# Latents' rows first, the recurrence's first rounds beside the last row chunks, and the input's eight tiles fetched at once

## The chip, the cores and the metric

The program runs on one core of a Trainium2 chip. The metric is the device time of one execution in microseconds (us). Names of engines: PE (TensorE: matmuls and transposes), DVE (VectorE), ACT (ScalarE), POOL (GpSimd), SP (SyncE, which here only issues DMAs). Each engine works off its own instructions in the order in which they were written; semaphores make one wait for another. ACT and POOL issue some DMAs too.

## What is computed

Two transformer blocks in float32 over 1024 tokens of width 1024. The change lies in the first part of the first block alone:

```
mod = silu(c) @ ada_w + ada_b                         # 6 x 1024
sh_m, sc_m, g_m, sh_f, sc_f, g_f = split(mod, 6)
h = rms_norm(x, mix_pre_norm) * (1 + sc_m) + sh_m
proj = h @ w_in                                       # 1024 x 2280
att_p, rwkv_p = proj[:, :456], proj[:, 456:]
y_att  = dsa_attention(c_q, c_kv, idx_k, idx_w ...)   # from att_p; picks the 256 best keys of each row
y_rwkv = rwkv7_group(rwkv_p, ...)                     # a recurrence over the tokens
mix = concat(y_att, y_rwkv) @ w_out
```

Inside `dsa_attention` an index score over all earlier tokens is computed (8 heads, relu, weighted sum), and the 256 largest of each row are kept. Inside `rwkv7_group` each row of `rwkv_p` is mixed with the row before it (`p + mu_shift * (p_prev - p)`), then split into r, k, v (512 columns each) and three narrow inputs of low-rank products (64, 64 and 160 columns, "lora" below), and a state of 8 heads x 64 x 64 is carried over the tokens. Everything behind it (attention proper, the feed-forward layers, the second block) is as before.

## The kernel before, in words

Tokens are worked in 8 tiles (t = 0 to 7) of 128 rows. The stages around the change, in PE's order:

1. **Opening.** `proj_scalar` fetches tiles of x into three buffers `xt`, three at once and each further one when its buffer is free; SP fetches 8 slices of `ada_w` (1 MB each, "mod" steps) into a ring of five slots (`ring_load`, L408). ACT squares and sums a tile, DVE scales it, PE transposes it into `hT` (L528) and multiplies a mod slice (L473). When all eight are through, DVE and ACT scale and shift the rows of `hT` (L724, L960).
2. **Lora**: 48 matmuls of 512 columns (L552) from `hT`; DVE mixes the result with the token before, ACT takes tanh.
3. **att and chunk 0**: per tile 8 matmuls of 256 and 8 of 200 columns (`token_group`, L508) for the attention's latents, then 8 x 8 for the first of six 256-column chunks ("rkv", 0 to 5) of r, k, v.
4. **Turns and index queries** (`LAT_STEPS`), with the first six row steps of chunk 1 between them.
5. **Scores** (`SCORES`, 24 steps): PE makes two heads (L618), ACT takes relu (`rl`, L1019), DVE adds them up (L913).
6. **Row steps** (`ROW_STEPS` from index 6 on): 34 row steps (8 matmuls of 256 columns each, one tile of one chunk) and 16 mod steps, 12 between row steps and 4 behind the last. Beside them DVE and ACT count, for six tiles and 33 candidates, how many scores exceed a candidate (`best_rows`, `best_sums`). That work is cut into 223 steps; `passes_beside` says how many are taken at each row step. Finished chunks go by POOL's DMA to `p_rows` in HBM.
7. **Recurrence.** Behind the last row step SP fetches eight broadcast rows (`rwkv_constants`), waits for the last chunk in HBM, and fetches tile 0 (`rows_load`). All engines meet (`rwkv_start`). Then 82 rounds follow: round g holds round g - 7t of each tile t, of the 33 rounds that a tile has. Rounds 0 to 6 are a tile's front (`front_*`), 7 to 20 its free part (`free_*`), 21 to 32 its part with the state (`state_*`). Beside rounds 0 to 29 two or one steps of `best_rows` are taken (`best_steps`).

## Time and profile before

| | us |
|---|---|
| median of 3 runs | 3683.32 (3676.62 to 3688.82) |
| profiled execution, its own time | 3676.93 |
| its span, first to last instruction | 3675.6 |
| PE busy | 3362.3 (91%) |
| DVE busy | 1789.6 (49%) |
| ACT busy | 931.7 (25%) |
| POOL busy | 345.4 (9%) |

In the page's line of 40 slices PE is at nine tenths or more from the tenth slice (920 us) on, nearly without a break; the slices before it read 6989757888. The attention proper begins at 895.8 us. Only what lies ahead of it is touched.

### The profile page before, as it was taken

The page shows a single profiled execution, that of the slowest core. Times are in us where ns is not written, and L with a number is a line of the kernel's source. Part 1 is how long each engine was busy: PE and PEld are TensorE (multiplying, and loading weights), DVE is VectorE, ACT ScalarE, POOL GpSimd, SP SyncE. Part 2 cuts the span into 40 slices and gives each one's busy share as a digit, 9 for nine tenths or more (in the row PEclk, how much of TensorE's full clock was granted, in tenths as well). Part 3 has the DMA queues.
Part 4 walks back from the last instruction along what each step waited for, and adds up shares of the span by engine and source line. Part 5 has one row for each costly group of instructions (what it writes and reads, how often), then busy time and mean ns, then how long its engine had stood idle before and what let it go on. Part 6 is the DMA issues. An engine that isn't in the chain of part 4 may idle for free.

```text
span 3675.6 us, 51037 instructions
## 1 busy us (share of the span) xinstructions
PE 3362.3 (91%) x21635; PEld 2614.7 (71%) x21650; DVE 1789.6 (49%) x2849; ACT 931.7 (25%) x1710; POOL 345.4 (9%) x277
## 2 busy tenths in 40 slices
PE   6989757888889999999999889999998999999998
PEld 3757546765557788888886556876676888878876
DVE  2248878663566422223544546322246444444556
ACT  2146532332543300001112435000015111111122
POOL 0000156662000000000000000000000000000000
PEclk8999877988999999999999999999999999999999
DMA  6145411110024111112340101101123111123434
GB/s 210 41 68 183 155 36 37 37 60 19 13 75 138 58 46 52 46 50 94 107 140 25 36 24 35 46 21 49 57 98 117 55 47 46 52 69 98 143 113 145
DMA packets 216068, 270.18 MB, mean 74 GB/s; under 512 B 11068, under 2 KB 176226, under 8 KB 215587
## 3 DMA queue, kind: packets, MB, share of 16 engines
q1 hardware_dynamic: 210555, 247.87, 21.1%
q10 hardware_dynamic: 3192, 11.17, 1.7%
q0 software_dynamic: 2096, 7.87, 0.6%
q8 instruction: 173, 2.83, 0.3%
q14 instruction: 52, 0.43, 0.0%
HBM read 232.80 MB, written 34.08 MB: 73 GB/s over the span
## 4 chain that ended last, share of the span: by engine, by line
PE 80%; DVE 11%; ACT 3%; issue 3%; DMA 2%; POOL 1%; SPq 0%; DVEq 0%; ACTq 0%; POOLq 0%
PE psum L1977 18%; PE psum L1981 18%; PE psum L1979 18%; PE psum L508 5%; PE psum L2995 3%; PE psum L1181 2%; PE psum L2495 2%; PE psum L2816 2%; PE psum L2703 2%; PE psum L552 1%; PE psum L1727 1%; PE psum L2832 1%; DVE scores L913 1%; PE psum L1753 1%; DVE Lg L1821 1%
## 5 line engine op out<-in xcount | busy, mean ns | idle before, releaser
L1977 PE MATMUL psum<-hT_hi,wcut_lo 128*128 128x512 f32 x1856 | 589.9, 395 | 16.8 <-DVE hT_lo L2016 16.8
L1981 PE MATMUL psum<-hT_lo,wcut_hi 128*128 128x512 f32 x1856 | 582.8, 391 | 0.0
L1979 PE MATMUL psum<-hT_hi,wcut_hi 128*128 128x512 f32 x1856 | 582.6, 391 | 0.0
L1977 PEld LDWEIGHTS psum<-hT_hi,wcut_lo 128*128 128x128 f32 x1856 | 350.7, 189 | 97.2 <-DVE hT_lo L2016 17.9
L1959 DVE CAST wcut_hi<-raw 128x1024 fp32r<-128x1024 f32 x256 | 177.1, 692 | 477.0 <-PE psum L1981 453.0
L1979 PEld LDWEIGHTS psum<-hT_hi,wcut_hi 128*128 128x128 f32 x1856 | 350.7, 189 | 73.0
L1981 PEld LDWEIGHTS psum<-hT_lo,wcut_hi 128*128 128x128 f32 x1856 | 350.4, 189 | 73.4
L1977 PE MATMUL psum<-wcut_hi,xcut_lo 128*128 128x512 f32 x1120 | 347.3, 391 | 17.6 <-DVE xcut_lo L2095 13.8
L1981 PE MATMUL psum<-wcut_lo,xcut_hi 128*128 128x512 f32 x1120 | 346.5, 391 | 0.0
L1979 PE MATMUL psum<-wcut_hi,xcut_hi 128*128 128x512 f32 x1120 | 346.2, 390 | 0.0
L1035 POOL TENSOR_TENSOR st<-st,nhalf 128x1 f32<-128x1 f32 (+2 forms) x78 | 61.0, 789 | 2890.0 <-DVE st L676 2890.0
L1961 DVE TENSOR_TENSOR wcut_lo<-raw,wcut_hi 128x1024 fp32r<-128x1024 f32 x256 | 313.8, 1226 | 8.8
L1977 PEld LDWEIGHTS psum<-wcut_hi,xcut_lo 128*128 128x128 f32 x1120 | 211.2, 189 | 63.4 <-DVE xcut_lo L2095 15.7
L1981 PEld LDWEIGHTS psum<-wcut_lo,xcut_hi 128*128 128x128 f32 x1120 | 211.1, 188 | 44.2
L1979 PEld LDWEIGHTS psum<-wcut_hi,xcut_hi 128*128 128x128 f32 x1120 | 211.1, 188 | 44.1
L508 PE MATMUL psum<-slot,hT 128*128 128x256 f32 (+1 forms) x1024 | 224.2, 379 | 4.2 <-DMA slot<-in_w_in 4.2
L508 PEld LDWEIGHTS psum<-slot,hT 128*128 128x128 f32 x1024 | 193.5, 193 | 33.9 <-issue 5.9
L2066 ACT ACTIVATE xcut_hi<-fS 128x512 fp32r<-128x512 f32 x88 | 55.1, 632 | 327.8 <-PE psum L1981 323.8
L2401 ACT ACTIVATE fS<-psum 128x1024 f32<-128x1024 f32 x22 | 22.6, 1029 | 428.8 <-PE psum L1981 428.8
L2392 DVE TENSOR_TENSOR fS<-fS,psum 128x1024 f32<-128x1024 f32 x22 | 26.9, 1221 | 190.9 <-PE psum L1981 190.9
L822 ACT ACTIVATE counted<-counted 128x1024 bf16<-128x1024 bf16 (+2 forms) x99 | 93.0, 942 | 69.9 <-DVE counted L804 69.9
L2427 DVE SCALAR_TENSOR_TENSOR tb<-psum,CF,tb 128x1023 f32<-128x1023 f32 x22 | 28.2, 1283 | 135.4 <-ACT tb L2447 135.4
(427 smaller groups left out, 4396.8 us busy)
## 6 DMA issues: line engine op xcount, KB each, us to landing
raw<-in_w_ffn_down SPq DMA_DIRECT2D x88, 512.0 KB, 3.6
raw<-in_w_ffn_up SPq DMA_DIRECT2D x66, 512.0 KB, 3.8
slot<-in_ada_w SPq DMA_DIRECT2D x24, 1024.0 KB, 11.2
raw<-in_w_in SPq DMA_DIRECT2D x28, 512.0 KB, 5.3
raw<-in_w_ffn_gate SPq DMA_DIRECT2D x22, 512.0 KB, 3.9
slot<-in_w_in SPq DMA_DIRECT2D x8, 1024.0 KB, 6.4
raw<-in_w_out SPq DMA_DIRECT2D x16, 512.0 KB, 3.7
x_one<-xrow SPq DMA_DIRECT2D x16, 512.0 KB, 2.8
```

The lines of the kernel that those rows point to most:

```text
L508: mm = pe.matmul(p[:, 0:n], K.hT[:, k, t * 128:(t + 1) * 128], w[:, k, 0:n], start=k == 0, stop=k == 7, skip_group_check=True)
L822: s.activation(a, a, ACT.Copy, accum_out=K.top[:, 0, t - 2:t - 1]).then_inc(*K.S.up(("counted", n, t)))
L1181: mm = pe.matmul(b0[par][half(c), cols64(q, o)], lhs(c, q, par), rhs(c, q, par), start=start, stop=stop, skip_group_check=True)
L1959: v.tensor_copy(hi, raw).then_inc(*K.V.up())
L1961: v.tensor_tensor(lo, raw, hi.bitcast(F), SUB).then_inc(*K.V.up(("cut", name, n)))
L1977: pe.matmul(outs[i], al, bs[i][0], start=start, stop=False, skip_group_check=True)
L1979: pe.matmul(outs[i], ah, bs[i][0], start=False, stop=False, skip_group_check=True)
L1981: mm = pe.matmul(outs[i], ah, bs[i][1], start=False, stop=stop, skip_group_check=True)
L2495: mm = pe.matmul(bank(K, t)[:, 0:n], K.hT2[:, k, t * 128:(t + 1) * 128], w[:, k, :], start=k == 0, stop=k == 7, skip_group_check=True)
L2703: mm = pe.matmul(bank(K, b)[:, 0:n], xT[:, k, t * 128:(t + 1) * 128], w[:, k, :], start=k == 0, stop=k == kt - 1, skip_group_check=True)
L2816: mm = pe.matmul(bank(K, b, 2)[:, o:o + n], K.qT[0:96, h, t * 128:(t + 1) * 128], K.kT2[0:96, h, o:o + n], start=True, stop=True, skip_gro ...
L2995: mm = pe.matmul(bank(K, b, 2)[:, h], K.wo[q % 2][j][:, k, :], xT[:, k, h], start=k == 0, stop=k == 3, skip_group_check=True)
```

## The change

It does five things.

- **x.** All eight tiles have a buffer (`xt` of NT) and are fetched at once by ACT; the four broadcast rows `GB`, `nrow` are fetched after `hT` is scaled. The first att group waits for each row of `hT` by itself, and ACT scales three rows of it, DVE five.
- **Order of the projection.** The att groups come first. The lora matmuls are cut: those of m = 0 one by one beside the first 16 score steps, those of m = 1 and 2 behind the scores. For that the scores have three pairs of PSUM banks (`score_bank`) where they had four. Beside the lora matmuls DVE and ACT take 30 steps of `best_rows`.
- **Mod steps.** All 16 lie between row steps, one for each from (1, 5) to (3, 4), with slots given by a table (`SLOT_OF`).
- **The front of tile 0.** Its rounds 0 to 6 lie beside the last 16 row steps, every second one from the fourth on (`round_beside`). The rounds of the recurrence begin with 7. r and k of tile 0 are fetched when chunk 3 is in HBM, its v apart and later (`keys_load`, `values_load`); the last chunk is stored in two halves. Of later tiles the v part of the front goes from round 1 to round 6. The broadcast rows are fetched earlier, the last three of them behind the others.
- **Steps of best_rows.** 170 lie ahead of the recurrence (172 before), and 3 are taken beside each of rounds 7 to 13, 2 beside each of 14 to 29.

Its core (buffers, semaphores and renamed addresses left out; `lo`, the region of `muB`, `prev` and `rowB` before, now holds the recurrence's `MK`, `XX`, `TX`, `RR`):

```diff
-ROW_LOADS = [("mod", j, q) for j in (0, 1) for q in range(4)] + ["lora a", "lora b", "att a", "att b", ("rkv", 0), ("rkv", 1),
-             "idx q"]
+ROW_LOADS = [("mod", j, q) for j in (0, 1) for q in range(4)] + ["att a", "att b", ("rkv", 0), "idx q", ("rkv", 1), "lora a", "lora b",
+             ("rkv", 2)]
...
-        if _c < 5 and _t in (5, 6, 7)[:3 if _c < 4 else 2]:
-            ROW_STEPS.append(_mods.pop(0))
+        if (1, 5) <= (_c, _t) < (3, 5):
+            ROW_STEPS.append(_mods[sum(s[0] == "mod" for s in ROW_STEPS)])
...
+BESIDE = len(ROW_STEPS) - 2 * NT
...
     for n, (t, q) in enumerate(SCORES):
-        score_tensor(pe, K, t, q, SCORE_BANKS[n % 2])
+        score_tensor(pe, K, t, q, n)
+        if n < 16:
+            lora_tensor(pe, K, 0, n)
+    for m in (1, 2):
+        for n in range(16):
+            lora_tensor(pe, K, m, n)
     for i in range(ROWS_FIRST, len(ROW_STEPS) + 1):
...
+        if round_beside(i) is not None:
+            front_tensor(pe, K, 0, round_beside(i))
+
+
+def round_beside(i):
+
+    n = i - BESIDE
+    return (n - 3) // 2 if n >= 3 and n % 2 and i < len(ROW_STEPS) else None
...
 def passes_beside(i):
-    return 4 if ROW_STEPS[i - 1][0] == "rkv" else 2
+    return 4 if ROW_STEPS[i - 1][0] == "rkv" and i <= BESIDE else 2
...
-    for t in range(3):
+    for t in range(NT):
         s.dma_start(K.xt[t], x_in[t * 128:(t + 1) * 128, :]).then_inc(*D[f"x{t}"].up(t, 16))
...
+        if step in (("rkv", 5, 3), ("rkv", 5, 7)):
+            a = step[2] - 3
+            g.wait_ge(*S.at(step))
+            g.dma_start(K.pd[1 + a * 128:1 + (a + 4) * 128, 1280:1536].rearrange("(t p) c -> p t c", p=128),
+                        K.stage[0][:, a:a + 4, :]).then_inc(*D["st2" if a else "st0"].up((5, a // 4), 16))
...
 def best_steps(g):
 
-    return 2 if g < 21 else 1
+    return 3 if g < 14 else 2
...
-    for g in range(STEP * (NT - 1) + LAST):
+    for g in range(STEP, STEP * (NT - 1) + LAST):
```

PE's order at the scores, where `iqT` and `ikT` are the score matmuls and `hT,slot` of 512 columns a lora matmul. Before:

```order
L618 MATMUL psum<-ikT,iqT 128x512 x18
L618 MATMUL psum<-ikT,iqT 128x384 x2
L618 MATMUL psum<-ikT,iqT 128x512 x2
```

and after the change:

```order
L651 MATMUL psum<-ikT,iqT 128x512 x4
L623 MATMUL psum<-hT,slot 128x512
L651 MATMUL psum<-ikT,iqT 128x512 x4
L623 MATMUL psum<-hT,slot 128x512
L651 MATMUL psum<-ikT,iqT 128x512 x4
L623 MATMUL psum<-hT,slot 128x512
```

One lora matmul stands behind each score step. Before, all 48 stood ahead of the att groups.

PE's order at the end of the row steps: `slot,hT` x8 is one row step, `slot,csz` a mod step, `wlo,lora` to `ident,brow` are the front of a tile, `aT,bT` is its round 7. Before:

```order
L508 MATMUL psum<-slot,hT 128x256 x64
L473 MATMUL psum<-slot,csz 32x256 x16
L492 MATMUL psum<-mrow,sel 128x256
L473 MATMUL psum<-slot,csz 32x256 x8
L492 MATMUL psum<-mrow,sel 128x256
L473 MATMUL psum<-slot,csz 32x256 x8
L492 MATMUL psum<-mrow,sel 128x256
L473 MATMUL psum<-slot,csz 32x256 x8
L492 MATMUL psum<-mrow,sel 128x256 x2
L1447 MATMUL psum<-wlo,lora 128x512 x2
L1452 MATMUL psum<-sig,mk 128x512
```

and after:

```order
L523 MATMUL psum<-slot,hT 128x256 x48
L1539 MATMUL psum<-wlo,lora 128x512
L523 MATMUL psum<-slot,hT 128x256 x16
L1539 MATMUL psum<-wlo,lora 128x512
L523 MATMUL psum<-slot,hT 128x256 x16
L1544 MATMUL psum<-sig,mk 128x512
L523 MATMUL psum<-slot,hT 128x256 x16
L1549 MATMUL psum<-mk,sig 128x2 x4
L523 MATMUL psum<-slot,hT 128x256 x32
L1560 MATMUL psum<-ident,Pe 128x128 x4
L1560 MATMUL psum<-ident,Pm 128x128 x4
L523 MATMUL psum<-slot,hT 128x256 x16
```

Tile 0's front went in between the row steps, and the mod steps away from the end.

POOL's order after the last three whole-chunk stores before the front (`p_rows<-stage` is a store of a chunk):

```order
L1128 DMA p_rows<-stage 128x8x256 x3
L1666 TENSOR_TENSOR prev<-prev,mx 128x1024
L1668 TENSOR_TENSOR prev<-prev,muB 128x1024
L1128 DMA p_rows<-stage 128x8x256
L1680 TENSOR_TENSOR sm<-sm,cst 128x8
L1682 TENSOR_TENSOR tmp<-mx,krow 128x512
L1684 TENSOR_TENSOR tmp<-tmp,rowB 128x512
L1123 DMA p_rows<-stage 128x4x256
L1689 TENSOR_TENSOR brow<-kk,aa 128x512
L1692 TENSOR_TENSOR brow<-brow,Pi 128x512
L1123 DMA p_rows<-stage 128x4x256
```

The stores of chunks 4 and 5 now stand behind POOL's share of front rounds 0, 3 and 4, where before all five stores stood ahead of the first `prev`.

## Rows read from the trace of the kernel before

**Rows 1.** Stretches: span, busy (instructions) of PE, PEld, DVE, ACT, POOL; PEclk, DMA, GB/s
```profile
0.00:65.90 65.90, 30.66 (x227) 20.11 (x228) 17.39 (x46) 22.15 (x38) 8.63 (x16) 0.81 0.90 292
...
230.50:279.20 48.70, 34.48 (x161) 14.95 (x160) 40.57 (x44) 34.50 (x47) 2.32 (x5) 1.00 0.48 51
279.20:422.80 143.60, 138.72 (x776) 115.42 (x778) 123.39 (x344) 91.38 (x204) 4.75 (x5) 0.98 0.53 171
...
444.10:481.80 37.70, 11.21 (x95) 7.71 (x96) 23.26 (x33) 10.63 (x21) 17.70 (x11) 0.51 0.11 42
...
530.90:577.60 46.70, 33.82 (x788) 29.41 (x788) 43.41 (x48) 13.87 (x21) 28.88 (x17) 0.85 0.11 36
577.60:625.00 47.40, 38.25 (x882) 34.37 (x880) 41.81 (x46) 14.76 (x23) 33.65 (x20) 0.78 0.10 36
```

**Rows 2.** The chain that ended last, 0 to 1000 us: start, length, what
```profile
36.52 6.33 DMA xt<-in_x
...
65.92 44.43 PE psum L552 x96
...
422.83 10.72 DMA p_rows<-stage
434.55 9.43 DMA prev<-p_rows
```

**Rows 3.** Timeline of the opening: start, length, engine, line, operation, [idle before <-releaser]
```profile
7.80 28.43 SPq L408 DMA_DIRECT2D slot<-in_ada_w  x8
...
21.39 1.94 PE L473 MATMUL psum<-slot,csz 128*32 128x256 f32 x16
...
58.47 1.07 PE L473 MATMUL psum<-slot,csz 128*32 128x256 f32 x16
...
61.18 2.98 DVE L724 TENSOR_SCALAR hT<-hT,AB 128x1024 f32<-128x1024 f32 x4
```

**Rows 4.** DMA in 0 to 80 us: GB/s in 40 slices of 2 us
```profile
GB/s 14 242 389 402 203 388 402 293 347 350 348 348 348 360 375 349 358 373 340 358 361 95 342 393 39 269 37 16 305 370 341 353 127 8 0 0 0 0 0 0
```

**Rows 5.** Timeline of the scores' first steps
```profile
234.48 9.62 DVE L913 SCALAR_TENSOR_TENSOR scores<-rl,iw,scores 128x1024 f32<-128x1024 f32 x7 [0.16 <-ACT rl L1019]
...
234.69 1.99 PE L618 MATMUL psum<-ikT,iqT 64*128 64x512 f32 x8 [0.50 <-ACT rl L1019]
...
235.80 1.02 ACT L1019 ACTIVATE rl<-psum 128x1024 f32<-128x1024 f32 x1 [0.42 <-PE psum L618]
```

**Rows 6.** PE's groups, 302 to 422 us: busy, mean ns | idle before
```profile
L508 PE MATMUL psum<-slot,hT 128*128 128x256 f32 x494 | 109.5, 381 | 0.0
```

**Rows 7.** Timeline of the row steps: a late weight tile, and first compares of two passes
```profile
294.43 6.65 PE L508 MATMUL psum<-slot,hT 128*128 128x256 f32 x16 [4.16 <-DMA slot<-in_w_in]
...
397.89 1.88 DVE L804 TENSOR_SCALAR counted<-scores,top 128x1024 bf16<-128x1024 f32 x3
...
422.60 2.18 DVE L804 TENSOR_SCALAR counted<-scores,top 128x1024 bf16<-128x1024 f32 x3
```

**Rows 8.** Timeline: a compare alone, and tile 0's rounds 6 to 9
```profile
427.49 0.75 DVE L804 TENSOR_SCALAR counted<-scores,top 128x1024 bf16<-128x1024 f32 x1
...
473.33 1.09 PE L1468 MATMUL psum<-ident,krow 128*128 128x128 f32 x4 [0.78 <-ACT rT L1556]
...
480.08 1.22 DVE L1258 TENSOR_TENSOR MK<-psum,mk 128x1024 f32<-128x1024 f32 x1 [7.84 <-PE psum L1199]
...
485.17 2.34 POOL L1566 TENSOR_TENSOR prev<-prev,mx 128x1024 f32<-128x1024 f32 x1
...
487.57 2.91 DVE L804 TENSOR_SCALAR counted<-scores,top 128x1024 bf16<-128x1024 f32 x1
```

**Rows 9.** DVE's groups, 530 to 625 us
```profile
L881 DVE TENSOR_TENSOR_SCAN rank<-tied,top 128x384 f32<-128x384 bf16 (+5 forms) x6 | 12.4, 2068 | 0.2
```

**Rows 10.** The end of the recurrence: a load behind round 69, and the chain into the attention
```profile
867.36 0.38 SPq L1151 DMA_DIRECT2D slot<-in_w_uq  x1
...
895.84 6.31 PE psum L1697 x8
```

More of the change, by code:

```diff
@@ L221, in dma @@
             K.D[n] = Signal(nc, f"landed_{n}")
-    dma("misc", "rows", "gb", "x0", "x1", "x2", "m2", "prows", "st0", "st1", "spill", "rb", "mu", "raw", "prev", "attw", "bias", "hot",
+    dma("misc", "rows", "gb", *[f"x{t}" for t in range(NT)], "m2", "prows", "st0", "st1", "spill", "rb", "mu", "raw", "prev", "late", "st2", "attw", "bias", "hot",
         "toep0", "toep1", "toep2", "toep3", "mk", "pos", "wo0", "wo1", "grow", "pp")
@@ L403, in ring_load @@
 def ring_load(sp, K, key, src, kt, cols):
-    i, before = K.ring.put(key)
+    i, before = K.ring.put(key, SLOT_OF.get(key))
     if before is not None:
@@ L538, in proj_tensor @@
     B.until(0, V, "modulation 0")
-    pe.wait_ge(*V.at(("hT", 7)))
-    pe.wait_ge(*S.at(("hT", 6)))
-    for m, (key, a, M) in enumerate((("lora a", 0, 128), ("lora a", 128, 128), ("lora b", 0, 32))):
-        w, landed = ring_tile(K, key, 8, 256 if key == "lora a" else 32)
-        b = 2 + 2 * m
-        pe.wait_ge(*landed.at(key))
-        pe.wait_ge(*B.free(b))
-        pe.wait_ge(*B.free(b + 1))
-        p = bank(K, b, 2)
-        for k in range(8):
-            for half in range(2):
-                h = slice(half * 512, (half + 1) * 512)
-                mm = pe.matmul(p[0:M, h], w[:, k, a:a + M], K.hT[:, k, h], start=k == 0, stop=k == 7, skip_group_check=True)
-        mm.then_inc(*T.up(("lora", m)))
-        if m:
-            T.mark(("free", key))
-        B.until(b, S, ("lora", m))
-        B.until(b + 1, S, ("lora", m))
     wa, la = ring_tile(K, "att a", 8, 256)
@@ L598, in proj_tensor, with lora_tensor, score_bank, score_tensor @@
             mod_sum(pe, K, ROW_STEPS[i - 1], ROW_BANK[i - 1])
-SCORE_BANKS = (2, 4), (6, 0)
-def score_tensor(pe, K, t, q, bs):
+        if round_beside(i) is not None:
[3 more added lines that the diff above has]
+    return (n - 3) // 2 if n >= 3 and n % 2 and i < len(ROW_STEPS) else None
+LORA = ("lora a", 0, 128, 6), ("lora a", 128, 128, 2), ("lora b", 0, 32, 4)
+def lora_tensor(pe, K, m, n):
+    key, a, M, b = LORA[m]
+    w, landed = ring_tile(K, key, 8, 256 if key == "lora a" else 32)
+    k, half = divmod(n, 2)
+    h = slice(half * 512, (half + 1) * 512)
+    if n == 0:
+        pe.wait_ge(*landed.at(key))
+    if k == 0:
+        pe.wait_ge(*K.bank.free(b + half))
+    mm = pe.matmul(bank(K, b + half)[0:M, :], w[:, k, a:a + M], K.hT[:, k, h], start=k == 0, stop=k == 7, skip_group_check=True)
+    if n == 15:
+        mm.then_inc(*K.T.up(("lora", m)))
+        if m:
+            K.T.mark(("free", key))
+        K.bank.until(b, K.S, ("lora", m))
+        K.bank.until(b + 1, K.S, ("lora", m))
+def score_bank(n, j):
+    return 2 * ((2 * n + j) % 3)
+def score_tensor(pe, K, t, q, n):
     T, V, S, B = K.T, K.V, K.S, K.bank
+    bs = score_bank(n, 0), score_bank(n, 1)
     W = (t + 1) * 128
@@ L765, in proj_vector @@
     K.best = best_rows(v, K)
+    for m, steps in enumerate(LORA_PASSES):
+        shift_vector(v, K, m)
+        for _ in range(steps):
+            next(K.best)
     for i in range(ROWS_FIRST, len(ROW_STEPS) + 1):
+        if i == ROWS_FIRST + 4:
+            for m in (1, 2):
+                L = K.lora[0:(128, 128, 32)[m], m, :]
+                v.wait_ge(*S.at(("gate tanh", m)))
+                v.tensor_scalar(L, L, 0.5, 0.5, MUL, ADD).then_inc(*V.up())
         for _ in range(passes_beside(i)):
@@ L989, in proj_scalar @@
         for j in range(2):
[L990 removed]
+            score_scalar(s, K, t, 2 * q + j, score_bank(n, j), 2 * n + j)
+        if n == 16:
+            lora_scalar(s, K, 0)
     K.sums = best_sums(s, K)
+    for m, steps in enumerate(LORA_PASSES):
+        if m:
+            lora_scalar(s, K, m)
+        low_scalar(s, K, m)
+        for _ in range(steps):
+            next(K.sums, None)
     for i in range(ROWS_FIRST, len(ROW_STEPS) + 1):
@@ L996, in proj_scalar, with lora_scalar, low_scalar @@
             next(K.sums, None)
+        if round_beside(i) is not None:
+            front_scalar(s, K, 0, round_beside(i))
+def lora_scalar(s, K, m):
+    M, b = LORA[m][2:]
+    s.wait_ge(*K.T.at(("lora", m)))
+    s.activation(K.lora[0:M, m, :], bank(K, b, 2)[0:M, :], ACT.Copy).then_inc(*K.S.up(("lora", m)))
+def low_scalar(s, K, m):
+    L = K.lora[0:(64, 128, 32)[m], m, :]
+    s.wait_ge(*K.V.at(("shift", m)))
+    s.activation(L, L, ACT.Tanh, scale=0.5 if m else 1.0).then_inc(*K.S.up(("gate tanh", m)))
 def lat_scalar(s, K, step, b):
@@ L1445, in front_tensor @@
         r = half(j)
+        if t == 0 and j == 0:
+            pe.wait_ge(*K.D["mk"].at("mk"))
+            pe.wait_ge(*S.at(("gate tanh", 0)))
         pe.wait_ge(*B.free(7))
@@ L1583, in front_pool @@
         g.wait_ge(*V.at(("unit", t)))
+        if t == 0:
+            g.wait_ge(*D["spill"].at("out"))
         g.tensor_tensor(K.bt[t % 4], K.kk, K.aa, MUL).then_inc(*G.up())
```

241 lines of the change are left out of this document (128 added, 113 removed).

## The prediction, made before the changed kernel ran

> **What bounds the kernel now.** I read the stretches first [rows 1]. From 895.8 us on the work is untouched, so only the first quarter counts, and in it each stage has another limit. In the opening PE is busy for 30.7 of 65.9 us while DMA is busy to 0.90 at 292 GB/s: a DMA stage. In the scores DVE has 40.6 of 48.7 us and PE only 34.5. In the row steps PE is bound (138.7 of 143.6) and DVE is not far (123.4). Then comes a hole: from 422.8 to 481.8 no full engine can be named; the stretch from 444.1 has PE at 11.2 us of 37.7 and its clock at 0.51. From 530.9 to 577.6 DVE is the full one (43.4 of 46.7).
>
> The chain of waits says what ends each stage [rows 2]. In the opening it is the fetch of one x tile after another (6.3 us, four such pieces one behind the other). Then the 48 lora matmuls, 44.4 us. Behind the last row step it is the last chunk's way to HBM (10.7 us) and back (9.4 us), and then tile 0's front, alone until its round 7, whose first product `MK` is masked at 480.1 [rows 8]. The last row step ends at about 422. So 58 us lie between them.
>
> **The opening.** Before, mod slices are issued until 36.2 us, the last is used at 58.5 and `hT` is scaled from 61.2 [rows 3]; PE starts on lora at 65.9 [rows 2]. After the change x no longer waits for buffers, and what is left is bytes. x (4.2 MB) and eight mod slices (8.4 MB) at some 350 GB/s [rows 4], from 2 us on: 12.6 / 0.35 = 36 us, so the last slice lands near 38.5. The slices that need a free slot are issued from 23.3 us on (the first is used by then [rows 3]), while earlier ones are still under way, so the queue does not run dry. The way from the last slice's product to the scaling is 2.7 us before (58.5 to 61.2), so scaling starts near 41.5. The first att group waits row by row and starts one row later, but it also needs both att slices, 1.9 MB more, 5.4 us: 44 to 45.5. I take 45.5. Bounds: 42 (rate 390, as in the best slices of [rows 4]) to 54 (the mean 292 GB/s of [rows 1] over 14.5 MB, and 4 us of start).
>
> **att to the index queries.** The same instructions, from lora's end at 110.3 [rows 2] to the scores' start at 230.5 [rows 1]: 120.2 us, which PE fills. The shifts and tanh that went were beside PE's att groups. Scores start at 45.5 + 120.2 = 165.7.
>
> **Scores.** 48.7 us before. Per step of 1024 columns DVE takes 2 x 1.37 us (9.62 us for 7) and PE 1.99 for its part [rows 5]; one lora matmul adds 44.4 / 48 = 0.93, so PE needs 2.9 where DVE needs 2.75. With three bank pairs PE can begin a step only when ACT has read the first half of the step before: 0.5 of latency, 1.4 for PE's first half and 1.0 for ACT [rows 5] against 2.75, about 0.2 over. I add 5 us in all (bounds 0 and 12: 0.5 for each of 24): 53.7, end at 219.4. So the first third of lora, 14.8 us, costs 5.
>
> **Lora 1 and 2** stand on PE alone: 32 x 0.93 = 29.6. Of the lora's 44.4 us only 14.8 - 5 = 10 are saved; the rest is moved behind the scores, where DVE would be behind anyway.
>
> **Row steps.** The trace has 34 row steps and 12 mod steps in 143.6 us. A row step is 16 records: 494 records take 109.5 us [rows 6], so 3.55 each, 120.7 for 34. With 4.2 us of a late weight tile [rows 7], 18.7 are left for 12 mod steps: 1.56 each. After: 120.7 + 16 x 1.56 = 145.7. Tile 0's front adds its PE work: most of the 11.2 us of [rows 1], at half clock there; I take 7.
>
> DVE's side: 170 steps. A pass of six takes (422.6 - 397.9) / 5 = 4.9 us at PE's pace [rows 7], of which some 0.3 is idle. By 4.7 a pass, 138 of the steps, three lora shifts (2.7 each), eight mod rows (0.9 each) and 5 us of sign work come to 128 us up to the 16th step from the end, while PE has 29.6 + 18 x 3.55 + 25 = 118.5. So DVE falls behind by up to 10 us, and since each mod product waits for ACT's copy of the one before, which stands behind ACT's counting, PE is held: 6 us. Further on DVE has 25 us of passes and 20 of front against PE's 64, and catches up; I add 2 for front rounds that wait. The late weight tile: rkv 4 is followed in SP's queue by the spill, the masks and the broadcast rows, some 5 MB or 15 us, before the last three mod slices are issued, six steps (17 us) ahead of need; I give it nothing of its own, it lies inside DVE's delay. Sum from the end of the scores: 29.6 + 145.7 + 7 + 8 = 190.3, so the last row step ends at 409.7 (422 before). Bounds of the 8: 0 and 25.
>
> Here a rule bears. With POOL at work on `prev` (485.2, 2.34 us) a compare that takes 0.75 us alone takes 2.91 [rows 8]. The Trainium skill (SBUF — State Buffer, "SBUF: two separate sides") says that DVE in its two-port modes and POOL take an exclusive lock for a whole instruction; the trace agrees. It speaks against the change, which puts POOL's front beside DVE's passes. By the lock each POOL instruction could hold DVE for its whole length.
>
> In this kernel's numbers: the compare above lost 2.2 us to a POOL instruction of 2.3, and tile 0's front has about nine on POOL, so at most 15 us; DVE's slack there is 64 - 45 = 19 minus the 10 that it is behind. I keep the 8 and give the rest to a rival.
>
> **The hole.** After the last row step come the second half of round 6 and round 7's products: `MK` is masked at +7 us, as before from the transposes of `krow` at 473.3 to 480.1 [rows 8]. So 416.7 for 480.1: 63 us earlier. This is the main term: 13 us of it come from the end of the row steps moving, 50 from the hole. v of tile 0 comes from the first half of chunk 5, stored four row steps (14 us) before the end; POOL mixes it behind tile 1's `prev`, where it did tile 1's v before, so it is there at round 9. The second half's store (5 to 10 us) is waited for by POOL's `T1` at +11. Where this cover is gone, it costs up to 9.
>
> **Rounds 7 to 29.** 53 steps of `best_rows` lie in 23 rounds, where before 37 did. Rounds 7 to 13: 21 counting steps for 14, +6 us of DVE, some 4 seen. Rounds 14 to 20, where DVE is full [rows 1]: 8 counting and 6 of the long last kind for 14 long ones; the long ones are 1.2 to 2.1 us ([rows 9] has the longest kind), so -4. Rounds 21 to 27: 14 long for 7, +11 of DVE, against 5.6 idle of 47.4 [rows 1]: +7. Rounds 28 and 29: +2. The v part of the front at round 6 rather than 1 evens POOL's load: -2 (bounds -14 and +5). Sum: 7 us lost. At the end, the latents' return and two weights are now issued behind round 69, at 867.4 [rows 10], 28 us before the attention starts at 895.8: 3.1 MB, 9 us, hidden.
>
> **Sum.** -63 + 7 = -56. The profiled execution: 3676.9 - 56 = 3621. The median of the runs shown is 6.4 us above that execution, which gives 3627. I take 3623.
>
> **Rivals.**
> - *DVE bounds the row steps.* Passes, shifts, front and the shared port keep PE waiting for 20 us more. For it: DVE at 123.4 of 143.6 us before, and more work. Against: 30 steps moved beside lora. Time 3643.
> - *More is gained.* The coupling and the score banks cost nothing (-13), POOL's evened load gives 1.5 us per tile (-10): 3600.
> - *The opening is not shortened*, because the slices are late when x takes the engines first: start at 58, +12: 3635. Against: [rows 4] shows 340 to 400 GB/s only while much is queued.
> - *Slower: the clock falls in the row steps.* Front rounds put waits between PE's row steps; in the hole, where PE waited between short pieces, the clock was 0.51 [rows 1], the lower of the two levels (1.2 GHz). There a mod product takes 1.94 us for 1.07 [rows 3]. From the scores' end to the last row step, 175 us of matmuls, that is +0.81 x 175 = 142 us; it eats the gain if over two fifths of the stretch is at the low level. Against: before, the clock stayed at 0.98 there in spite of a 4.2 us wait [rows 7], and in the scores with PE at 71% it was 1.00. Time if all of it: 3765; at the point from which it decides: 3683.
>
> The Trainium skill (TensorE: Matmul & The Clock Gate, "HAM oscillation — how this bites in real kernels") tells of a loop whose wait in front of each burst lets the clock fall again every time; by it the last 16 row steps are in danger. The hole agrees, the row steps before speak against it.
>
> **Chances.** The forecast's case 0.60 (3608 to 3638), DVE bound 0.16, more gained 0.12, opening not shortened 0.08, clock 0.04. Beyond 0.3% (11 us, about what a measurement of this kernel can tell from no change), that gives faster 0.94, same 0.02, slower 0.04. The range that leaves out 2 in 10: 3592 to 3652.
>
> **What would show it.** Right: PE's first att group at 43 to 48 us; scores from 163 to 168 and 50 to 56 us long; the last row step ending at 400 to 418, its clock over 0.95; `MK` of tile 0 masked 6 to 10 us later; its groups of rounds 21 to 27 longer than 47.4 us, by 4 to 10; the attention at 830 to 850. Wrong: a first att group behind 52, PE waiting for `mrow` or `sig` for over 15 us in the row steps, or a low clock there; a wait for `prevV` or the second half's store over 5 us; the attention's start held by its loads.

## The result, and the profile after

The changed kernel takes 3645.67 us (median of four runs, 3641.48 to 3651.53), the kernel before 3679.97 (median of four): ratio 0.9915, 95% interval 0.9897 to 0.9932. It is faster by some 34 us. A second set of six runs gives 3648.07 and 0.9926 (0.9907 to 0.9944). Forecast were 3623 and a range of 3592 to 3652: the sign and the range hold, the gain is three fifths of the 56 us of the sum. The profiled execution has a span of 3645.5 us, 30 less than before: 28 of them lie ahead of the attention, 2 behind it.

The stretches of the changed kernel, with the columns of [rows 1]: opening, pass over the latents, scores, second and third part of the lora, row steps (in three lines: up to the last modulation slices, the wait for them, from there to the first front round beside a row step), row steps with the front, what is left until `MK`, and the attention:

```profile
0.00:46.70 46.70, 22.85 (x228) 15.41 (x228) 17.19 (x46) 20.77 (x37) 8.64 (x16) 0.99 1.03 335
...
169.70:233.50 63.80, 55.93 (x193) 20.71 (x192) 42.31 (x46) 34.41 (x49) 1.46 (x5) 0.89 0.46 57
233.50:274.00 40.50, 34.78 (x104) 14.53 (x108) 34.83 (x87) 20.51 (x39) 1.34 (x1) 0.92 0.24 78
274.00:333.70 59.70, 59.30 (x411) 45.32 (x411) 56.08 (x156) 41.69 (x96) 1.79 (x2) 0.97 0.78 264
333.70:347.20 13.50, 2.90 (x14) 2.21 (x12) 9.19 (x26) 3.17 (x7) 0.00 (x0) 0.70 1.03 338
347.20:385.00 37.80, 37.78 (x195) 30.56 (x196) 24.69 (x68) 21.04 (x47) 0.95 (x1) 0.93 0.37 121
385.00:440.10 55.10, 49.78 (x221) 41.43 (x220) 34.78 (x69) 21.49 (x46) 14.03 (x9) 0.94 0.21 72
440.10:444.30 4.20, 2.65 (x73) 2.16 (x72) 0.41 (x2) 2.61 (x5) 0.79 (x1) 1.00 0.37 129
...
867.70:3645.00 2777.30, 2644.37 (x12282) 2061.84 (x12297) 1251.24 (x1943) 614.02 (x1127) 50.34 (x70) 0.98 0.22 70
```

The line that stands out is 333.7 to 347.2: PE has 2.9 us of work in 13.5, while DMA is full at 338 GB/s. The opening now ends at 46.7, with DMA at 335 GB/s where [rows 1] had 292. Its chain of waits shows two long fetches one behind the other and then PE, in place of the four x tiles of [rows 2]:

```profile
22.11 12.87 DMA slot<-in_ada_w
34.98 11.60 DMA slot<-in_w_in
...
46.67 1.62 PE psum L523 x3
```

What PE waited for between 169 and 445 us (engine, line, what released it: us in all, times, longest):

```profile
PE psum L483 <- DMA slot<-in_ada_w: 10.6, 1, 10.6
PE psum L651 <- ACT rl L1081: 6.4, 11, 0.8
PE psum L508 <- ACT mrow L494: 5.4, 1, 5.4
PE psum L1560 <- ACT aT L1654: 5.3, 1, 5.3
```

The first is the modulation slices of the long empty line above. SP's timeline says why they are late. The last three slices are the row at the bottom; above it stand the twelve transfers of `rwkv_weights`, each of which keeps SP for 0.5 to 1.9 us:

```profile
320.94 0.37 SPq L419 DMA_DIRECT2D slot<-in_w_in  x1
321.43 0.51 SPq L1169 DMA_DIRECT2D latents<-spill  x1
...
325.89 1.06 SPq L1178 DMA_DIRECT2D rowB<-in_w  x1
...
331.77 1.90 SPq L1179 DMA_DIRECT2D muB<-in_mu_shift  x1
333.72 10.44 SPq L419 DMA_DIRECT2D slot<-in_ada_w  x3
```

And the masks of the first products of tiles 0 to 4, seven rounds apart, which answer to the 480.08 of [rows 8]; first before, then after (start, length, and in brackets how long DVE was idle before and what ended that):

```profile
480.08 1.22 DVE L1258 TENSOR_TENSOR MK<-psum,mk 128x1024 f32<-128x1024 f32 x1 [7.84 <-PE psum L1199]
529.79 1.23 DVE L1258 TENSOR_TENSOR MK<-psum,mk 128x1024 f32<-128x1024 f32 x1 [0.65 <-PE psum L1199]
...
674.98 1.23 DVE L1258 TENSOR_TENSOR MK<-psum,mk 128x1024 f32<-128x1024 f32 x1 [0.67 <-PE psum L1199]
```

```profile
444.30 1.22 DVE L1343 TENSOR_TENSOR MK<-psum,mk 128x1024 f32<-128x1024 f32 x1 [3.79 <-PE psum L1284]
497.89 1.23 DVE L1343 TENSOR_TENSOR MK<-psum,mk 128x1024 f32<-128x1024 f32 x1 [0.65 <-PE psum L1284]
547.34 1.23 DVE L1343 TENSOR_TENSOR MK<-psum,mk 128x1024 f32<-128x1024 f32 x1 [0.89 <-PE psum L1284]
606.52 1.23 DVE L1343 TENSOR_TENSOR MK<-psum,mk 128x1024 f32<-128x1024 f32 x1 [0.92 <-PE psum L1284]
665.01 1.23 DVE L1343 TENSOR_TENSOR MK<-psum,mk 128x1024 f32<-128x1024 f32 x1 [0.67 <-PE psum L1284]
```

The first mask is 35.8 us earlier, the fifth only 10.0, and the attention starts at 867.7 where it started at 895.8, 28.1 earlier. So the recurrence loses 26 us in its first four tiles and has 18 back at its end.

### The profile page after: what moved, and what is told of

It is laid out like the page before. It is cut to its first block, busy times and chain, and to the rows that moved or that the text cites. A ratio compares the mean times of both kernels' runs of the same rounds, so it can differ in the third digit from the quotient of the medians.

```text
span 3645.5 us, 51038 instructions
## 1 busy us (share of the span) xinstructions
PE 3346.4 (92%) x21635; PEld 2602.0 (71%) x21650; DVE 1794.3 (49%) x2850; ACT 928.1 (25%) x1709; POOL 339.0 (9%) x278
## 4 chain that ended last, share of the span: by engine, by line
PE 81%; DVE 11%; ACT 4%; issue 2%; DMA 1%; POOL 1%; SPq 0%; DVEq 0%; ACTq 0%; POOLq 0%
PE psum L2071 18%; PE psum L2073 18%; PE psum L2075 18%; PE psum L523 5%; PE psum L3089 3%; PE psum L1266 2%; PE psum L2589 2%; PE psum L2910 2%; PE psum L2797 2%; PE psum L651 1%; PE psum L1821 1%; PE psum L2926 1%; DVE Lg L1915 1%; PE psum L1847 1%; DMA slot<-in_ada_w 1%
## 5 line engine op out<-in xcount | busy, mean ns | idle before, releaser
L2073 PE MATMUL psum<-wcut_hi,xcut_hi 128*128 128x512 f32 x1120 | 347.2, 392 | 0.0
L2160 ACT ACTIVATE xcut_hi<-fS 128x512 fp32r<-128x512 f32 x88 | 55.1, 632 | 329.8 <-PE psum L2075 325.8
```

Source lines behind the costliest of these rows:

```text
L2073: pe.matmul(outs[i], ah, bs[i][0], start=False, stop=False, skip_group_check=True)
```

## The experiments

Each group of runs has the kernel before beside it, and a ratio is taken to that. Its medians in the four groups lie between 3673.97 and 3679.37 us, so medians from different groups can be compared only to within some 6 us. In the expectations e2 is the lora behind the scores, e7 the changed kernel with two edits, e10 the steps spread otherwise.

**The transfers ahead of the slices.** Edit, in the loop of loads on SP:

```diff
-        if key == ("rkv", 4):
+        if key == MODS[-1]:
             rwkv_weights(sp, K)
```

> Undoes nothing; it moves the issue of the recurrence's weight slices (rwkv_weights) in the row stretch from behind the issue of ('rkv', 4) to behind the issue of the last modulation slice, so that SP's twelve transfers of 320.9 to 332 us stand behind the slices and no longer ahead of them. Theory (SP's order): in the changed kernel PE waited 10.62 us at 347.21 us for the last modulation slices, which SP could issue only at 333.72 us behind those twelve issues; the wait goes, and with it part of the cold clock behind it (0.70 in the stretch 333.7 to 347.2 us). The time is 10 to 14 us below the changed kernel's 3645.7, ratio to before about 0.988. Rival (bandwidth or slots): the slices wait for their buffers or for the 338 GB/s that all transfers of the stretch share; then the same bytes come just as late and the recurrence's weights later still: a change within 3 us, or a wait at the recurrence's start instead.

Measured: 3630.30 us (3626.67 to 3637.02), ratio 0.9873 (0.9857 to 0.9890), 15 us below the changed kernel. The last three slices are now issued at 320.14 us and the broadcast rows behind them:

```profile
320.14 10.53 SPq L419 DMA_DIRECT2D slot<-in_ada_w  x3
...
338.65 0.46 SPq L1178 DMA_DIRECT2D rowB<-in_a  x1
```

PE's wait for a slice is gone from its list of waits, and the row steps up to the last one run at a clock of 0.98:

```profile
270.70:424.10 153.40, 147.09 (x841) 118.22 (x842) 125.19 (x320) 87.19 (x196) 16.72 (x12) 0.98 0.56 188
```

The order in SP's queue is the cause. The engines are as full as before and carry the same bytes, but the slices are issued 13.6 us earlier (333.7 to 320.1); the mask of tile 0 comes at 428.3 for 444.3 (2 of these 16 us were there already at the end of the scores), and the recurrence did not wait for the weights that now come later. Slots are not the cause. Whether a slice was late by the issues ahead of it or by their bytes, this run leaves together; a later one takes them apart. The fall of 15 us is one more than the upper end expected.

**The bytes or the issues.** Edit to the changed kernel: of the twelve transfers, only the first, the latents' store of 2 MB, goes behind the last slice; the eleven small ones (2.7 MB) stay ahead.

> The changed kernel with one transfer moved: the latents' store (2 MB, one issue) goes behind the last modulation slice, the eleven smaller transfers of the recurrence's weights (2.7 MB, eleven issues) stay ahead of the slices. It tells apart what the first experiment left together: whether a slice was late by the bytes ahead of it or by the time that SP takes for the issues. By bytes: at 338 GB/s the 2 MB are 6 us, so PE's wait of 10.6 us for the slices falls to about 4.6. By issues: only 0.5 of the 12.8 us goes, and the wait stays at 10 us; the issues would take 1.0 to 1.1 us each, as in the changed kernel. If the issues themselves get shorter (0.45 us, as behind the slices in the first experiment), their length was the transfers' pressure and not their own.

Measured: 3651.71 us (3647.99 to 3652.11), ratio 0.9931 (0.9902 to 0.9961), no gain in time that could be told from the changed kernel's. PE's wait is 7.4 us, between the 4.6 of the bytes and the 10 of the issues:

```profile
PE psum L485 <- DMA slot<-in_ada_w: 7.4, 1, 7.4
```

SP issued the eleven in 8.1 us (316.53 to 324.68), and the slice behind them took 14.33 us to land:

```profile
316.53 0.55 SPq L1172 DMA_DIRECT2D wlo<-in_w_decay_up  x1
...
322.00 1.64 SPq L1179 DMA_DIRECT2D rowB<-in_k_a  x1
323.69 0.46 SPq L1179 DMA_DIRECT2D rowB<-in_r_k  x1
324.18 0.45 SPq L1180 DMA_DIRECT2D muB<-in_mu_shift  x1
324.68 11.14 SPq L419 DMA_DIRECT2D slot<-in_ada_w  x3
```

The same kind of broadcast row (`rowB`) is issued in 0.46 to 1.64 us, so the length of an issue is not its own. The slice is late by both, but not by equal parts. From the issue of the weight tile ahead of the twelve to the slice's landing it is 12.9 us in the first experiment, 23.0 here and 26.2 in the changed kernel. The landing itself takes 11.4, 14.3 and 13.5 us; so 2 to 3 us of the lateness are landing, and the rest, 7.2 here and 11.3 in the changed kernel, is time in which SP was issuing other transfers. Neither theory alone gives the 7.4.

From the end of the scores to the mask of tile 0 this kernel needs 208.0 us for 211.2, just the 3.2 that the wait is shorter. That these 3 us are not seen in the time is no contradiction: behind the mask this profile was slower by 8.9 us up to the attention (432.3 for 423.4), as the second profile of the changed kernel is (431.4, below).

**The lora beside the scores.** Edit: the 16 matmuls of the first third go back behind the scores, and the scores alternate between `(2, 4)` and `(6, 0)` again:

```diff
-        if n < 16:
-            lora_tensor(pe, K, 0, n)
-    for m in (1, 2):
+    for m in (0, 1, 2):
...
-    return 2 * ((2 * n + j) % 3)
+    return ((2, 4), (6, 0))[n % 2][j]
```

> Undoes one part of the change: the first third of the lora stands behind the scores again, as before, and the scores have their four pairs of banks again. Theory (the overlap hid nothing: with three pairs of banks the scores' steps are 3.32 us apart, set by PE loop, ScalarE's pass and back): scores 48 to 51 us (63.8 in the changed kernel), lora 44 to 45 us (28.8), and the 5.4 us for which PE waited for ScalarE's mrow at 273.0 us go at least in part, since VectorE and ScalarE catch up during the first third; sum -6 to 0 us against 3645.7. Rival (the overlap is worth what it was made for, and the slow steps come from the cold clock alone): +8 to +12 us, 3655 or more.

Measured: 3653.91 us (3645.47 to 3659.16), ratio 0.9937 (0.9920 to 0.9953). By its stretches (scores, first third) the profile says that one behind the other costs what side by side cost, 64.0 us for 63.8:

```profile
169.10:219.10 50.00, 34.54 (x162) 14.93 (x161) 41.75 (x46) 35.50 (x48) 2.33 (x5) 1.00 0.51 63
...
219.10:233.10 14.00, 14.00 (x33) 6.34 (x34) 1.28 (x3) 0.49 (x2) 0.29 (x1) 1.00 0.24 34
```

The attention starts 1.1 us earlier than in the changed kernel (866.6). My side point fell: PE waited 6.8 us for `mrow`, not less than 5.4. The timed runs lie nearer to the rival, with an interval that overlaps the changed kernel's. The profile is of the fastest of the six executions (3645.47); three of them took 3657 to 3659, and of those there is no profile. So the profile and the times do not say the same here, and this run alone decides nothing.

**The front behind the row steps.** Edit: `round_beside` gives `None`, and the recurrence's loop starts at round 0 again, with two steps of the row work a round and then one.

> Undoes one part of the change: no round of the recurrence stands beside the last row steps; the rounds 0 to 9 of the first tile follow the row steps, as before, and each later round carries the steps of the row work that it carried before. Theory: the stretch without PE work between the last row step and the first round of all heads (about 62 us before, of it about 35 to 43 us front rounds that the change moved beside the row steps) comes back, less the about 7 us that the front's matmuls cost PE in the row steps and the about 7.6 us that the rounds lost: slower than the changed kernel by 25 to 40 us, ratio to before 0.998 to 1.003. Rival (the opening gave the gain, and the front's share is eaten by the waits that it brings into the row steps): slower by less than 12 us.

Measured: 3663.81 us (3661.39 to 3668.59), ratio 0.9964 (0.9952 to 0.9977). That is 18 us slower, under the 25 to 40 of the theory and over the 12 of the rival. Row steps with all that is ahead of them, and the hole:

```profile
228.20:421.90 193.70, 175.79 (x913) 129.02 (x913) 143.88 (x389) 101.96 (x223) 5.73 (x6) 0.95 0.48 160
421.90:460.20 38.30, 13.08 (x95) 8.19 (x95) 27.63 (x44) 16.01 (x31) 13.47 (x8) 0.55 0.13 42
```

The hole is 38.3 us long, where before it was 58. The missing 20 are the last chunk's way to HBM and back (10.7 and 9.4, [rows 2]): the front starts at 421.87 us, on the last row step's heels, although it is not beside it. So the new order of loads and stores alone takes the transfers out of the hole, and the front beside the row steps takes out 34 of the other 38, and costs the row steps 12.9 (206.6 for 193.7), of which 5.3 are the wait for `aT`. With 5.9 more in the rounds (423.4 for 417.5), 15 of the 34 stay. I had expected 25 to 40 because I took the whole hole for front. (18 us by the medians and 15 by this sum agree within the spread.)

**Steps given back.** Edit: three steps of the row work beside each of the last 16 row steps, and the former numbers beside the rounds:

```diff
-    return 4 if ROW_STEPS[i - 1][0] == "rkv" and i <= BESIDE else 2
+    return 2 if ROW_STEPS[i - 1][0] == "mod" else 4 if i <= BESIDE else 3
...
-    return 3 if g < 14 else 2
+    return 2 if g < 21 else 1
```

> Gives each of the last row steps three steps of the row work of VectorE and ScalarE in place of two, so that 16 steps are not left for the recurrence's rounds; each round carries one to two as before. Theory (the rounds' loss of 7.6 us between the first round of all heads and the attention is the price of those steps): that stretch falls from 423.4 to 416 to 419 us, the row steps stay as long as they are, and the time falls by 4 to 8 us. Rival (VectorE is as full beside the row steps as beside the rounds): PE waits in the row steps for sig and mrow by as much, the last row step ends 4 to 10 us later, and the time stays within 3 us of the changed kernel's.

Measured: 3637.29 us (3631.79 to 3641.98), ratio 0.9890 (0.9874 to 0.9906): 8 us faster. From the mask to the attention 414.2 us (446.2 to 860.4), 9.2 less, but the mask is 1.9 later, although the scores were 4 us shorter here (their last steps had the full clock, with no edit to them). The rival is right about a part: PE's wait for `aT` grew from 5.3 to 8.9, with another of 2.6 for `kT`.

**The opening alone.** Edit: the kernel before, with eight buffers for x, all fetched at once, and the broadcast rows issued behind the scaling.

> The kernel before with the opening's part of the change alone: eight buffers for x, all tiles fetched at once, the broadcast rows of the gates and norms issued behind the scaling. Nothing else moves. Theory (the opening is bound by the transfers, and what it gains is kept to the end because the stages behind it are bound by PE and VectorE): the first group of the pass that follows starts 16 to 20 us earlier, and so does every stage up to the attention; time -16 to -20 us, ratio to before 0.9945 to 0.9957. Rival (given back later: the weights of the row steps and the rows on their way to HBM still come at the pace of the transfers): the start of the row steps or the recurrence waits for them, and -8 us or less stays.

Measured: 3660.55 us (3653.64 to 3664.38), ratio 0.9953 (0.9936 to 0.9970), -14 us by the medians, -17 by the ratio. In its profile PE starts the lora at 48.50 us (65.92 before, [rows 2]) and the mask of tile 0 stands at 462.62 (480.08, [rows 8]). The first lora matmuls:

```profile
48.50 3.75 PE L552 MATMUL psum<-hT,slot 128*128 128x512 f32 x4 [5.27 <-ACT hT L955]
```

All 17.4 us of the opening are kept. This kernel and that with the front behind the row steps differ by all the rest of the change but the coupling of front and row steps, and their times are the same within the intervals: of the 20 us of transfers taken out of the hole, 17.5 went into two waits of the row region, 6.9 for `mrow` and 10.6 for the slices.

**The changed kernel once more, two edits together, and three.** The second kernel has two edits, that of "The transfers ahead of the slices" and that of "Steps given back"; the third has that of "The lora beside the scores" besides.

> The changed kernel as it is, beside the other three on one chip, since the profiles differ among themselves by about 5 us in the scores, where the last steps ran at 0.94 us in two kernels and at 1.67 us in two. Expected: 3641 to 3651, median 3646, ratio 0.9915. If the scores' last steps run at the fast level in this profile, the stretch of the scores is 59 to 60 us and no longer 63.8, with no edit to it.

> The changed kernel with two edits of the experiments before together: the recurrence's weight slices are issued behind the last modulation slice, and each of the last row steps carries three steps of the row work in place of two. Theory (the two have different causes, a late transfer and the load of VectorE): the gains add, -15 and -8 against the changed kernel, 3619 to 3627, ratio about 0.985. Rival (the row steps' VectorE work was hidden in the 10.6 us wait for the slices, and with the wait gone three steps beside each row step hold PE): 3630 or more, no better than the first edit alone.

> The same two edits and the third of e2_lora_behind: the first third of the lora behind the scores, with four pairs of banks. In the profile of e2 the scores and this third together took 64.0 us (50.0 and 14.0) against 63.8 side by side, yet its median was 8 us above the changed kernel's. Theory (side by side and one behind the other cost the same): within 4 us of the kernel with two edits, and the 8 us were the spread between executions. Rival (side by side keeps something that the one profile missed): 5 to 9 us slower than the kernel with two edits.

Measured: the changed kernel 3648.07 us (3641.18 to 3659.82), ratio 0.9926 (0.9907 to 0.9944); with two edits 3626.03 (3624.40 to 3628.49), 0.9862 (0.9844 to 0.9881); with three 3632.38 (3621.89 to 3635.78), 0.9866 (0.9845 to 0.9887). Within this group the two edits gain 22 us, near the sum of their single gains (15 and 8). Across the groups that is less sure: against the kernel before of its own group the first of the two edits alone stands at -49.1 us, both together at -48.9, and the intervals of the ratios overlap. What the steps add is seen in the profiles, from the end of the scores to the attention: 634.6 us in the changed kernel, 621.9 with the first edit, 613.7 with both, each with the full clock in the 15 us shown below.

With the first third of the lora behind the scores besides, the ratio is the same (0.9866 for 0.9862), the median 6 us higher, which the rival had named; the intervals overlap, and in its profile the mask of tile 0 comes at 437.7 for 437.1. So side by side is worth somewhere between nothing and 6 us, and no run decides it. Where spread comes from, the second profile of the changed kernel shows. It is of the slowest of its six executions: its span is 3658.5 us, 13 more with the same instructions and with scores and mask of tile 0 within 0.4 us of the first. Of the 13 us, 8 lie between that mask and the attention and 5 behind the attention's start, in whose first 50 us the clock was 0.84 where it was 0.96. Here are the 15 us that end 13 us before the attention, in the first and in the second profile:

```profile
839.70:854.70 15.00, 11.34 (x271) 8.68 (x268) 8.39 (x14) 3.40 (x6) 5.58 (x5) 1.00 0.61 209
```

```profile
847.40:862.40 15.00, 15.00 (x182) 11.17 (x184) 4.51 (x8) 1.19 (x2) 4.96 (x4) 0.50 0.79 279
```

At a clock of 0.50 (1.2 GHz) PE does 182 matmuls in 15 us, at 1.00 (2.4 GHz) 271 in 11.3. The stretch from the eighth mask to the attention takes 69.7 us in the one (from 798.05 to 867.7) and 76.5 in the other (798.88 to 875.4). The kernel before had the lower clock there in its profile, 0.59. The scores' last steps showed 1.67 us here again, not 0.94, so this expectation was not met in this run.

**Three pairs without the lora.** As in "The lora beside the scores", but with the changed kernel's banks, `2 * ((2 * n + j) % 3)`.

> As e2_lora_behind (the first third of the lora behind the scores), but with the changed kernel's three pairs of banks: it tells whether the scores' slow steps come from the banks or from the lora matmuls between them. Theory (banks: TensorE's whole step of 2.0 us, then ScalarE's pass over its first half, 1.03, then 0.25 until TensorE starts again): the first four steps, 1024 columns wide, stand 3.3 us apart though no lora matmul stands between them, where four pairs gave 2.4 to 2.8; the narrower ones at 2.9, 2.6 and 2.2; the scores take 56 to 60 us (50.0 with four pairs) and the first third 14 behind them. Rival (the lora matmuls make the steps long): the steps stay at 2.8 us and less, the scores at 50 to 52 us.

Measured: 3667.97 us in a single run, from which no ratio follows; what counts here are the rows. The chain through the first scores, start and length:

```profile
168.23 1.97 PE psum L649 x8
170.20 1.01 ACT rl L1076
171.21 0.24 issue
171.45 2.01 PE psum L649 x8
...
174.78 2.01 PE psum L649 x8
```

The steps stand 3.3 us apart with no lora matmul between them. The changed kernel has the same distance with a lora matmul between them:

```profile
169.75 1.97 PE psum L651 x8
171.71 1.01 ACT rl L1081
172.73 0.24 issue
172.97 2.01 PE psum L651 x8
```

That settles it: up to 206.5 us the steps start at the same distances, to 0.2 us, with and without lora matmuls between them. Three pairs of banks make the loop, PE's whole step, ACT's first pass, 0.3 us; the lora matmuls only fill the gaps. (ACT's first pass waits for the whole step because `score_tensor` writes its two heads in turns, so that both are ready at the end.) In this run the gaps had a second price. The scores took 68.7 us and not 56 to 60, since from 207 us on the clock was 0.50:

```profile
168.20:207.00 38.80, 23.07 (x107) 10.28 (x108) 26.81 (x26) 22.40 (x27) 0.88 (x3) 1.00 0.51 62
207.00:236.90 29.90, 21.69 (x57) 7.65 (x53) 15.43 (x21) 10.85 (x20) 0.59 (x2) 0.50 0.31 40
```

Until it fell PE had been busy for 23.1 of 38.8 us, at the full clock, with a gap of 1.3 in each step. The Trainium skill (TensorE: Matmul & The Clock Gate, "HAM oscillation — how this bites in real kernels") describes loops with a stall ahead of each burst, whose clock falls again every time. The trace agrees in part: the clock fell in such a loop, but only after 38.8 us of the same stalls at the full clock, and it then stayed low. With lora matmuls in the gaps and the banks as here, the last steps of the scores were at the full clock in four profiles and at the half clock in five, so it is not the loop alone that decides. The prediction weighed the same rule for the last row steps; there (385.0 to 440.1 above) the clock was 0.94.

**The steps spread otherwise.** As the kernel with two edits, the same 48 steps in another order, and that kernel again beside it:

```diff
-    return 2 if ROW_STEPS[i - 1][0] == "mod" else 4 if i <= BESIDE else 3
+    if i > BESIDE:
+        return 3 if i <= BESIDE + 4 else 4 if i <= BESIDE + 10 else 2
+    return 4 if ROW_STEPS[i - 1][0] == "rkv" else 2
```

> As e7_mods_and_steps, with the same 48 steps of the row work beside the last 16 row steps, but no longer three beside each: three beside the first four, four beside the next six and two beside the last six, where the front's last rounds stand. In e7 VectorE was busy for 19.8 of 28 us before 400 us, and TensorE then waited 8.9 us for aT and 2.6 for kT of the front. Theory (the front's chain waits because the row work stands in its way on VectorE and ScalarE): the wait for aT falls to about 5 us, MK comes 3 to 6 us earlier than e7's 437.1, the rounds behind it keep their 408.6 us: 3 to 6 us faster than the kernel with two edits. Rival (the front's own chain of small operations sets the wait): the waits stay, within 2 us of it.

> The kernel of e7_mods_and_steps once more, for the comparison with e10 on one chip. Expected: 3624 to 3629, ratio 0.985 to 0.988, MK at 436 to 438 us, and a second profile of the same instructions: the clock in the 15 us before the last 13 of the recurrence is either 1.00 as in e7 or about 0.6 as in the changed kernel's second profile, and where it is the lower the stretch from MK to the attention is 5 to 8 us longer.

Measured: 3621.67 us (3616.99 to 3628.16), ratio 0.9855 (0.9841 to 0.9869), against 3632.29 (3614.51 to 3633.44), 0.9864 (0.9843 to 0.9885), for the kernel with two edits. The mask of tile 0 comes at 430.5 us, 6.5 earlier, of which 3.0 are gained in the scores, whose last steps had the full clock in this profile. Of the front's waits the one of 8.9 for `aT` became one of 5.6, which now ends with an operation of the row work (`top`), and PE waits 6.8 for `mrow` where it was 4.5. The rounds behind the mask did not keep their 408.6 us: 413.9, at the lower clock at their end. The intervals overlap, so whether the new spread gains the 3 us is open. Either kernel is 1.4% below the one before, where the changed one is 0.7 to 0.9% below it. The repeated kernel's second profile had 0.59 in the 15 us where its first had 1.00, and took 411.9 us from mask to attention for 408.6: 3.3 more, less than the 5 to 8 expected.

## Why the prediction was right in sign and too large

Point by point, by its own terms (us; forecast, then the first profile after):

| term | forecast | measured |
|---|---|---|
| first att group | 45.5 | 46.7 |
| from there to the scores | 120.2 | 123.1 |
| scores with a third of lora | 53.7 | 63.8 |
| lora, row steps, front beside them | 190.3 | 206.6 |
| last row step to `MK` | 7 | 4.2 |
| `MK` to the attention, against before | +7 | +7.6 |

The differences (1.2, 2.9, 10.1, 16.3, -2.8, 0.6) add up to 28.3, and that is what the attention missed: 28.1 us earlier where 56 were forecast. The 2.9 of the second line are the clock for the most part: its first 5.7 us (46.7 to 52.4) ran at 0.50, where the same groups stood behind the lora before and had 0.99.

- **Opening: right.** The 17 to 19 us are there in both kernels that have it, and are kept to the end. The rival in which the slices come late fell.
- **Scores: the step that failed is the term of 5 us for three pairs of banks.** It is 15. I had counted PE's first half, ACT's pass and the latency against DVE's 2.75, but ACT starts its first pass only when PE's whole step is done (the chain above: 2.0 + 1.0 + 0.3 = 3.3). Of the 15, 11 are banks (59.7 us for 48.7, in the profile with the front behind the row steps, where the clock stayed at 1.00), inside the bounds of 0 and 12; 4 are the half clock of the last steps (63.8), which had no term.
- **Row region: the step that failed is "I give it nothing of its own, it lies inside DVE's delay".** The bytes were counted (5 MB, 15 us), the order was seen, and the need was put 17 us later; but in SP's queue twelve issues take 12.3 us before a slice can even start (321.43 to 333.72), it then takes 13.5 to land, and DVE's delay hides nothing of a transfer that PE needs afterwards. It cost 10.6 us of waiting, and 13.6 in all by the first experiment (row region 193 us for 206.6). The stalls for `mrow` and `aT`, 10.7 us, are what the term of 8 meant, and near it. The rival of DVE as the bound names a time (3643) near the measured one; its cause is not what happened.
- **The hole: right in what it is.** The 50 us that it was to give are 54 by the two runs that take it apart: 20 of transfers and 34 of front. The mask is 35.8 us earlier and not 63 because of the errors ahead of it.
- **Rounds: right in the sum, by luck; two errors cancel.** The first four tiles lose 26 us and not 9: from the first to the fifth mask 221 us, 195 before, and 204 in the kernel with two edits, which has 37 steps in these rounds (437.05 to 640.94). Tile by tile the changed kernel is 3.9, 2.8, 9.5 and 9.7 us longer than the one before, the kernel with two edits 4.5, 3.6, 0.6 and 0.4. So the added steps cost 18 us, all in rounds 21 to 34, where +7 and +2 were forecast, and nothing in rounds 7 to 20; the 7 us lost there are lost with 37 steps too and have another cause (for 3.3 of them, the wait for `vrow` below). The rest gains 18 and not 2. There the same 4290 matmuls take 169.5 us of PE for 182.2, at a clock of 0.93 for 0.87:

```profile
665.00:867.70 202.70, 169.51 (x4290) 142.23 (x4291) 124.58 (x154) 65.70 (x103) 131.24 (x91) 0.93 0.12 39
```

```profile
675.00:895.80 220.80, 182.23 (x4290) 152.27 (x4290) 122.96 (x154) 66.36 (x103) 132.97 (x91) 0.87 0.11 36
```

  About 5 to 7 of the 18 are the clock of the recurrence's last rounds, which changes between executions of one kernel (above). For the rest, 3 us a tile, I had named POOL's evened load; no run here took that apart, and it stays open. The kernel with the opening alone does not have it (140.0 us from the fifth mask to the eighth, 133.0 in the changed kernel), so it is not the opening.
- **The clock in the row steps: right that it did not decide.** 0.93 to 0.97, but for the wait for the slices (0.70); the sign asked for over 0.95.
- **A wait not seen:** PE waits 10.9 us for `vrow` behind the first mask (PE reaches its first product with `vrow` at 459.1, 14.8 us behind the mask; 11.6 before). It is POOL's chain, not the second half's store: from 445.6 to 459.0 us POOL goes without a gap through its part of the products, tile 1's `prev` and tile 0's `prevV`. Against before it costs 3.3 us. The prediction had `v` there in time at round 9, and it had named a wait for `prevV` of over 5 us as a sign that it was wrong.
- **Its signs.** Of those for being right, the first att group (46.7) and the longer rounds 21 to 27 (by 9.5) hold. The scores' start and length, the last row step (440.1 for 400 to 418), the mask (4.2 behind it) and the attention's start (867.7 for 830 to 850) lie outside. The time lies in its range, and the mechanisms are those forecast but for the two steps above.
- **A row misread.** The prediction put the compare of 2.91 us beside POOL's instruction at 485.17 [rows 8]; that one had ended when the compare began (487.57). Beside it stood POOL's next, and the one at 485.17 had another of DVE's beside it, which takes 0.17 us alone:

```profile
485.27 2.26 DVE L861 SCALAR_TENSOR_TENSOR top<-top 128x6 f32<-128x6 f32 x1
487.59 2.34 POOL L1568 TENSOR_TENSOR prev<-prev,muB 128x1024 f32<-128x1024 f32 x1
```

  What was made of it, that a DVE instruction can lose a whole POOL instruction, holds for both.

## What to carry to other kernels

A transfer is late by what stands ahead of it in its queue, by the issues and again by the bytes, so those with the nearest need go first: one moved line gave some 15 us. Before giving a stage fewer buffers to make room for work beside it, write down the loop that frees a buffer, with the instruction that really releases each engine; here the work beside came free and the loop cost as much as was saved. And when one profile and the timed runs disagree by 5 to 10 us, take a second profile of the same kernel before explaining either.

## What the runs showed of the hardware beyond that

- One kernel has, in the same stretch, a clock of 1.00 in one execution and 0.5 to 0.6 in another (the 15 us that end 13 us before the attention: 1.00 in seven of the profiles here, 0.50 to 0.60 in the seven others, the kernel before among these). Between two profiles of the changed kernel that was 8 us up to the attention and 5 behind its start; in the kernel with two edits 3 and 5.
- The issue of one and the same kind of broadcast row held SP for 0.45 to 1.64 us with the DMA engines full (a share of 0.93 to 1.03). What makes it longer, no run here shows.
- The Trainium skill (SBUF — State Buffer, "SBUF: two separate sides") had been weighed as a rule against the front beside DVE's passes. POOL was busy for 14 of the 55.1 us there and DVE for 34.8, and beside the front PE's longest wait was the 5.3 us for `aT`. What agrees with a lock is seen in two instructions of the kernel before, the compare of [rows 8] and the one at 485.27; how much of those 5.3 us is due to it, no run here tells.
